# Sums over channels on TensorE: one product of 128 tokens, or four of 32 tokens on the array's column quarters

## What is computed

```
def rmsnorm(x, g):
    y = xf * lax.rsqrt(jnp.mean(xf * xf, axis=-1, keepdims=True) + RMS_EPS)
def l2norm(x):
    return x * lax.rsqrt(jnp.sum(x * x, axis=-1, keepdims=True) + RMS_EPS)
...
    q = l2norm(q.astype(jnp.float32)) * (dk ** -0.5)
    k = l2norm(k.astype(jnp.float32))
...
            o_a = rmsnorm(o_a, even_dn_norm[e]) * jax.nn.silu(dn_gate.reshape(Bsz, S, DN_HEADS, DN_DV))
...
            o_b = (rmsnorm(o_b, even_diff_subln[e]) * (1.0 - lam_init)).reshape(Bsz, S, DIFF_V)
```

## Time and profile before

| | |
|---|---|
| median of 3 runs | 1417.47 us (1417.21 to 1417.5) |
| the profiled execution, its own time | 1416.82 us |
| its span, first to last instruction | 1415.1 us |
| TensorE busy | 1359.9 us, 96% |
| DVE, ACT, POOL busy | 816.3, 574.7, 124.0 us |
| mean granted TensorE clock | 0.975 of full speed |
| TensorE's share of the chain that ended last | 88% |
| line 721 | 160 product records, 2% of the chain |

### The profile page before, as it was taken

How to read it: one execution, slowest core, us unless ns; L and a number is a source line. 1 busy time by engine, 2 the same in 40 slices (tenths; PEclk the granted TensorE clock), 3 DMA queues, 4 the chain that set the end, 5 groups by cost and what they waited for, 6 DMA issues and landing times.

```text
span 1415.1 us, 21106 instructions
## 1 busy us (share of the span) xinstructions
PE 1359.9 (96%) x7795; PEld 1098.5 (78%) x7795; DVE 816.3 (58%) x1260; ACT 574.7 (41%) x794; POOL 124.0 (9%) x137
## 2 busy tenths in 40 slices
PE   7989989999899999999999999999999999999996
PEld 5868768777678888888888777777878888888885
DVE  4886675777656654355555555555656653355543
ACT  5522411465434452233334455554444442233342
POOL 1030030001121000000012001000210000000011
PEclk9999799999999999999999999999999999999998
DMA  8311010223235523333224332332323423433131
GB/s 257 90 45 48 15 47 1 75 57 119 71 107 162 154 74 89 104 112 96 67 78 127 90 82 69 91 88 74 90 60 94 113 67 93 125 95 96 56 93 59
DMA packets 218666, 124.93 MB, mean 88 GB/s; under 512 B 6063, under 2 KB 215450, under 8 KB 218356
## 3 DMA queue, kind: packets, MB, share of 16 engines
q1 hardware_dynamic: 213760, 112.52, 28.4%
q0 software_dynamic: 3664, 11.58, 2.9%
q10 hardware_dynamic: 1188, 0.08, 0.1%
HBM read 119.92 MB, written 9.48 MB: 91 GB/s over the span
## 4 chain that ended last, share of the span: by engine, by line
PE 88%; DVE 6%; ACT 3%; issue 1%; DMA 1%; ACTq 0%; POOL 0%; DVEq 0%; POOLq 0%
PE acc L699 72%; PE acc L1108 3%; PE R L977 2%; PE R L991 2%; PE R L831 2%; PE R L721 2%; DVE cta L1656 1%; PE R L1081 1%; ACT wh L416 1%; PE R L819 1%; PE R L1040 1%; PE R L880 1%; DVE wl L420 1%; DVE wl L1665 1%; DMA out<-ob 0%
## 5 line engine op out<-in xcount | busy, mean ns | idle before, releaser
L699 PE MATMUL acc<-mh,wh 128*128 128x512 f32 x1120 | 319.2, 405 | 3.3 <-ACT wh L1271 1.8
L699 PE MATMUL acc<-ml,wh 128*128 128x512 f32 x1120 | 313.3, 398 | 3.1 <-DVE ml L1582 3.1
L699 PE MATMUL acc<-mh,wl 128*128 128x512 f32 x1120 | 309.6, 396 | 0.1
L420 DVE TENSOR_TENSOR wl<-raw,wh 128x2048 fp32r<-128x2048 f32 (+1 forms) x103 | 222.1, 2156 | 118.2 <-ACT wh L416 118.2
L416 ACT ACTIVATE wh<-raw 128x2048 fp32r<-128x2048 f32 (+1 forms) x111 | 200.6, 1807 | 141.7 <-PE acc L699 141.7
L699 PEld LDWEIGHTS acc<-mh,wh 128*128 128x128 f32 x1120 | 207.4, 190 | 56.6 <-issue 12.0
L699 PEld LDWEIGHTS acc<-ml,wh 128*128 128x128 f32 x1120 | 211.7, 191 | 50.2 <-DVE ml L1582 4.6
L699 PEld LDWEIGHTS acc<-mh,wl 128*128 128x128 f32 x1120 | 211.8, 191 | 45.4 <-DVE wl L436 0.5
L565 POOL TENSOR_TENSOR ssum<-ssum,sq 128x512 f32<-128x512 f32 x32 | 49.9, 1559 | 747.1 <-ACT sq L1221 746.4
L2145 DVE SCALAR_TENSOR_TENSOR cta<-cb,pv,cta 128x512 f32<-128x512 f32 x88 | 66.1, 751 | 74.1 <-ACT cta L1520 67.7
L699 PE MATMUL acc<-ah,wl 128*128 128x512 f32 x352 | 98.0, 396 | 0.0
(11 more groups left out here) (314 smaller groups left out, 1544.2 us busy)
## 6 DMA issues: line engine op xcount, KB each, us to landing
raw<-in_ffn_w_in SPq DMA_DIRECT2D x88, 512.0 KB, 5.0
raw<-in_ffn_w_out SPq DMA_DIRECT2D x32, 384.0 KB, 4.0
raw<-in_even_w_in SPq DMA_DIRECT2D x23, 512.0 KB, 5.2
raw<-in_ffn_w_out SPq DMA_DIRECT2D x32, 320.0 KB, 3.7
raw<-in_odd_w_qkv SPq DMA_DIRECT2D x16, 512.0 KB, 4.6
rel_bias_extended<-rel_bias_rows POOLq DMA_DIRECT2D x16, 320.0 KB, 4.0
raw<-in_even_w_out SPq DMA_DIRECT2D x8, 512.0 KB, 4.7
raw<-in_odd_w_qkv SPq DMA_DIRECT2D x16, 256.0 KB, 3.1
```

The lines of the kernel that those rows point to most:

```text
L420: nc.vector.tensor_tensor(wl[s][:, 0:n], raw[s][:, 0:n], wh[s][:, 0:n].bitcast(F32), ALU.subtract).then_inc(sem(f"w_tail{s}"), 1)
L699: last = nc.tensor.matmul(acc[2 * s + t][:, :], ws[0 if form[0] else 1][:, t, k, :], mov[0 if form[1] else 1][:, k, :], start=form == HEAD ...
```

## The change

`token_sums` makes four products where it made one. Each takes 32 tokens as the stationary operand, sits on one column quarter of the array, and writes 32 partitions of the same result column. The moving operand is the same column of ones. Sums, operands and results are otherwise the same; 80 products become 320, so 160 records become 640.

```
             def token_sums(r, c0, squares):

                 for b in range(NB):
-                    last = nc.tensor.matmul(r[:, c0 + b:c0 + b + 1], squares[:, b * P:(b + 1) * P], ones[:, 0:1],
-                                            start=True, stop=True)
+                    for q in quarter:
+                        last = nc.tensor.matmul(r[q, c0 + b:c0 + b + 1], squares[:, b * P + q.start:b * P + q.stop],
+                                                ones[:, 0:1], start=True, stop=True, tile_position=(0, q.start))
                 return last
```

## The result

The kernel with the change took 1396.3 to 1400.2 us, the kernel before 1416.4 to 1417.5; the ratio is 0.987 (95% interval 0.985 to 0.989). One further execution of the changed kernel took 2972.6 us; it counts in the median of 1399.6, which is 1398.9 without it, and in nothing else here.

A forecast was written before the change was run, and what follows sets the result against it. TensorE, busy for 96% of the span, was taken as the bound. Terms of 2.0 + 5.4 + 1.0 + 1.6 + 1.1 + 1.2 = 12.3 us off the 1417.47 us median gave 1405.2 us, range 1400.0 to 1411.5.

The forecast's parts named there:

- The products: At all twenty sums: 32 small records 8.7 or 14 ns apart, saving 0.59 or 1.26 us a sum, less 0.2 a place.
- The rival of loads that follow one another: Column quarters share one path for weights, 27 ns a load at full clock: nothing saved, about 1420 us; chance 0.06.
- The rule on a floor of about 25 ns: At every small product: at least about 25 ns start to start, so 0.80 us a sum and about 1415 us.
- First pair: Four sums at 58 us: TensorE saves 2.2 us, then waits for DVE's diagonal; 2.0 us booked (1.0 to 3.0).
- Second pair: Sums at 153 and 165 us: TensorE saves 5.8 us, ACT is late next; 5.4 us booked (4.0 to 7.3).
- the route over ACT: At 153 to 167 us: ACT's second table load, and L1740 after it, come 5.1 us earlier.
- The outputs and the differential heads: Two sums at 256 us, 1.0 us with TensorE as bound; four differential heads at 0.4 us each, 1.6 us.
- Norm 1: The sum at 407 us, at half clock: 1.26 less 0.2 for the place, 1.1 us booked.
- Norms 2 to 4: Three single sums, 0.4 us each, 1.2 us booked; the last is all on the path.
- The fourth rival: At 62, 157 and 407 us one half-clock stretch each goes, 1.7 us apiece: 16.4 us, about 1401 us; chance 0.14.

The follow-up runs named there:

- by_quarter: The change with the loop over the quarters outside, so four products in a row sit on one column quarter: 1410.9 us, ratio 0.995.
- rest_only: The kernel before with quarters only at the four sums of the DeltaNet output and the four differential heads: 1408.7 us, ratio 0.995.
- before_again: The kernel before, unchanged, profiled once more: 1417.0 us.
- norm1_only: The kernel before with quarters only at norm 1 (407 us): 1413.2 us, ratio 0.998.
- norms_only: The kernel before with quarters only at the four norms of x: 1412.2 us, ratio 0.997.
- halves: The change with two products of 64 tokens on column halves in place of four on quarters: 1409.3 us, ratio 0.995.
- doubled: The change with each small product made twice, 1280 records: 1414.6 us, ratio 0.998.
- mixed_whole: The kernel before, whole sums, with groups of three projection products moved between the sums of q and k: 1422.2 us, ratio 1.0045.
- after_again: The change, unchanged, timed in more rounds and profiled again: 1399.3 us, ratio 0.988.
- qk_only: The kernel before with quarters only at the eight sums of q and k (58 and 153 us): 1409.5 us, ratio 0.995.
- wider: The change with column quarters also for the gate products and the four products of L782: 1402.3 us, ratio 0.990.
- early_fill: The change with three groups of the second pair's projection products moved ahead of its gate sums: 1401.1 us, ratio 0.990.
- mixed_quarters: The change with groups of three projection products moved between the sums of q and k: 1405.3 us, ratio 0.992.
- dense_fill: The change with one more float32 product of 288 columns ahead of each sum: 1408.4 us, ratio 0.994.
- whole_dense: The kernel before, whole sums, with one more float32 product of 288 columns ahead of each sum: 1428.1 us, ratio 1.009.

## Why the prediction was wrong, point by point

**The products.** Right. Forecast: 8.7 ns apart at full clock, 14 at half, 0.28 and 0.45 us a sum, 0.2 us for entering and leaving. Measured: 8.4 to 8.8 ns, and at half clock (0.60 - 0.17) / 31 = 13.9. The rival of loads that follow one another fell: by_quarter shows 22.6 ns where they must, 8.4 where they need not. The rule on a floor of about 25 ns from the Trainium skill (TensorE: Matmul & The Clock Gate, Part 1), which was set beside that rival, does not agree with the change: 8.4 ns. Even on one quarter alone it is 22.6 ns at full clock, and 34 at half.

**First pair, booked 2.0 us.** Right. L820 started at 62.45 us and waited 1.48 us for DVE's diagonal, as argued (forecast 62.6). DVE's L1800 started at 63.62 in place of 65.80, 2.2 us, of which 0.15 stood there before the first sum. What the clock gave to the projections behind the sums went into that wait. By the next pair's sums the shift is 153.13 - 150.18 = 2.95 us. The other 0.8 us came between 85 and 100 us, where no sum stands: before, the clock was at 0.50 for 3.4 us at 85.8 and again at 96.1, with the change for 6.8 us at 81.8, while TensorE was partly waiting. Nothing was booked for that; in the repeated profiles it is 1.4 us.

**Second pair, booked 5.4 us.** L1741 started 8.5 us behind the first sum (158.67 - 150.18) and not 13.5 (166.68 - 153.13), 5.1 us, to the tenth what the route over ACT gave. By the run of products of L830 at 183 us, which stood at 191.9, the pair had given 8.7 - 2.95 = 5.7 us. In the repeated profiles, where all four sums ran at full clock with the change, it gave 7.0.

**The outputs and the differential heads, booked 1.0 and 1.6.** From the sums at 256 us to norm 1 the shift grew from 9.8 to 12.9 us, 3.1 in place of 2.6; 1.0 us of it came at the half-clock stretch of 369 us, which got shorter. Between the second pair and these sums it had grown by another 1.1 us, for which nothing was booked. The repeated profiles say how little that is worth: there it shrank by 2.6 us over the same stretch, while the whole gain, 17.8 us, was the same.

**Norm 1, booked 1.1 us.** This term failed. Between norms 1 and 2 the kernel took 368.07 us before (406.71 to 774.78) and 364.55 after (393.81 to 758.35), 3.5 us less; the repeated pair of profiles gives the same 3.5. The sum itself went from 1.57 us (406.71 to 408.28) to 0.36, 1.1 with the entering, as booked. The other 2.4 are the projections behind it, which ran at half clock before and at full clock after. The prediction's sum took "at half clock" as a fixed property of that place and priced only the sum by it. It does not follow that the short sum alone lifts the clock there: in rest_only the place was at full clock with the whole sum.

**Norms 2 to 4, booked 1.2.** They gave 0.2, 0.7 and 0.6 us.

So the step that failed is the treatment of the clock in the added-up forecast: a gain from less half-clock work was booked for the sums and, by about 1 us, at the pairs, and put at nothing at norm 1, where it was 2.4 us, and everywhere else. The fourth rival, "the clock gives back more", at 1401 us and a chance of 0.14, is what came, and its own size was slightly short. 71 us at half clock became 45. As a rough estimate, twenty sums at full-clock prices and the twelve switches are 20 x 0.59 - 2.4 = 9.4 us, 26 us fewer at half clock are worth up to 13, and against them TensorE's waits grew: the 1.48 us is new, the 2.70 was 0.26, and the wait for ACT ahead of L830 at 83 us is 3.5 in place of 2.4. That leaves some 17, and the span fell by 17.9.

**What is shown of the clock, and what is not.** The profiles, by place:

- Behind the first pair's sums the clock fell in before, before_again, rest_only, norm1_only, norms_only, by_quarter, halves, doubled and mixed_whole. It did not in the change, after_again, qk_only, wider, early_fill, mixed_quarters, dense_fill and whole_dense. In the first nine the four sums take 1.8 us or more, in the next six they take 1.1 to 1.5 us. So short sums spare this drop. For wide products the record is divided: whole_dense has 288 columns, in two passes, ahead of each whole sum and no drop, mixed_whole has three products of 512 columns among its first three whole sums and a drop.
- At norm 1 the half-clock time is 6.8 us in four of the five profiles with a plain whole sum and none in rest_only; it is none in five of the eight with a sum on quarters in the change's order (one of them dense_fill), and 3.4 us in the other three. Short sums go with less of it, and do not decide it.
- At the second pair it is 17 to 20 us in four profiles with whole sums and 10 us in three; with sums on quarters it is 7 us in three, 10 us in early_fill and 17 to 20 us in three. Here the record does not show that short sums bring the clock back sooner. With the change it came back after TensorE had had nothing but wide products from 152.0 to 156.9 us, before after the same from 159.95 to 164.4; in rest_only and norm1_only it was up for 3.4 us ahead of the sums and in the first of them as well.

That waits and the place of the work against the clock share in all three is argued from these differences; no run varied either alone. Which part of the 4 to 6 us above the forecast is due to short sums and which to place was not separated. rest_only, with 42 us at half clock in all, as few as the change, says that place can do much: its profile gained 4.7 us at norm 1 and 1034.7 us with no edit at either.

## What to carry to other kernels

Here a product of 128 weight columns with one moving column took 0.109 us a record, and cutting it over the column quarters made a sum 2.4 times as fast (0.36 us for 0.88), provided that products next to each other lay on different quarters. When narrow work on TensorE is shortened, price the wide work behind it as well: look whether it ran at the lower clock, and expect some of that back. Where a kernel scatters by 9 us from one execution to the next, a variant that ought to give 1 us cannot be judged.

## What was not expected of the hardware

- The same 32 products take 0.36 us or 0.80 us by nothing but their order over the quarters.
- TensorE can stand still inside long runs of small products. With 256 in a row it stood for 2.5 us shortly before the end of the run (doubled), and in wider for 3.9 us inside L885, waiting for nothing that the profile shows. In halves and rest_only such idle time adds up to 5.8 and 5.0 us, in before and the change to 1.8 and 1.0. The page's DMA part has more packets on the instruction queue in the kernels with more instructions, in before, the change and doubled:

```profile
q8 instruction: 38, 0.62, 0.2%
```

```profile
q8 instruction: 42, 0.69, 0.2%
```

```profile
q8 instruction: 47, 0.77, 0.2%
```

That the idle time is a wait for instructions was not tested, and the packets do not settle it: halves and rest_only have 40, fewer than the 42 of the change.
- With one product of 288 columns ahead of each whole sum (whole_dense) the clock stayed high at the first pair and stayed low at the second.
